# A decoder layer with an expert gather: output products of the first token tile pulled ahead, the second group's depthwise convolution moved to ScalarE and GpSimd, its output products spaced out

## What is computed

```
h = x + W_out( concat[A, B, C, D]( rmsnorm(x) @ W_in ) )
x = h + PEER( rmsnorm(h) )                     then a final rmsnorm
A  convolution group: GLU, causal depthwise conv of width 31 over 256 channels, layernorm, swish
B  RWKV-7 time mixing (state update over chunks of 64 tokens)
C  short gated convolution, width 3
D  multi-scale causal pooling
PEER: 8 heads; for each token and head the 16 best of 128 x 128 product keys pick 16 experts;
      out = sum over the 128 picked experts of gate * gelu(u . x) * v,   u, v rows of 1024
```

## Time and profile before

| | |
|---|---|
| median of 3 runs | 1740.42 us (1735.06 to 1740.69) |
| the profiled execution | 1737.21 us |
| its span | 1735.4 us |
| DVE busy | 1269.9 us (73%) |
| PE busy | 1238.7 us (71%) |
| POOL busy | 911.6 us (53%) |
| ACT busy | 698.1 us (40%) |
| moved by DMA | 602.42 MB, 545.29 MB of it by GpSimd's gathers |
| chain that ended last | DMA 39%, PE 25%, DVE 16%, POOL 6%, issue 6%, ACT 4% |

### The profile page before, as it was taken

How to read it: one execution, slowest core, us unless ns; L and a number is a source line. 1 busy time by engine, 2 the same in 40 slices (tenths; PEclk the granted TensorE clock), 3 DMA queues, 4 the chain that set the end, 5 groups by cost and what they waited for, 6 DMA issues and landing times.

```text
span 1735.4 us, 19464 instructions
## 1 busy us (share of the span) xinstructions
PE 1238.7 (71%) x5360; PEld 623.9 (36%) x5360; DVE 1269.9 (73%) x2983; ACT 698.1 (40%) x1986; POOL 911.6 (53%) x1134
## 2 busy tenths in 40 slices
PE   5997898667767777767976757676767667677555
PEld 4886766323334343332322413232323223222110
DVE  3569755689888878768586778777777777777775
ACT  3321113455444444334345444343434343434444
POOL 0155120476676556544365656565656565556652
PEclk9999898878899898887987878787877787867778
DMA  5321147999999999999799999999999999999996
GB/s 173 122 100 47 37 138 95 319 397 412 418 410 416 417 405 419 417 418 392 260 374 417 419 417 419 415 401 417 417 409 404 418 411 418 409 408 410 418 419 254
DMA packets 110636, 602.42 MB, mean 347 GB/s; under 512 B 24752, under 2 KB 27184, under 8 KB 43968
## 3 DMA queue, kind: packets, MB, share of 16 engines
q0 software_dynamic: 74880, 545.29, 76.8%
q1 hardware_dynamic: 35648, 55.90, 11.0%
HBM read 597.96 MB, written 3.19 MB: 346 GB/s over the span
## 4 chain that ended last, share of the span: by engine, by line
DMA 39%; PE 25%; DVE 16%; POOL 6%; issue 6%; ACT 4%; DVEq 3%; POOLq 0%; SPq 0%; ACTq 0%
DMA arena<-in_uv,arena 38%; PE ps L981 9%; DVE arena L1844 8%; PE ps L551 4%; POOL arena L2068 4%; DVEq L1313 3%; DVE arena L1316 3%; PE ps L598 2%; POOL arena L2067 2%; PE ps L904 2%; DVE arena L1322 2%; PE ps L589 2%; PE ps L611 1%; ACT arena L1280 1%; PE ps L923 1%
## 5 line engine op out<-in xcount | busy, mean ns | idle before, releaser
L981 PE MATMUL ps<-arena 128*64 128x512 f32 x2048 | 666.9, 785 | 402.7 <-ACT arena L1280 401.8
L1844 DVE CUSTOM_DVE_ANT_0 arena<-arena 128x1024 f32<-128x1024 f32 x520 | 639.1, 1230 | 276.7 <-DMA arena<-in_uv,arena 247.5
L2068 POOL DMA_INDIRECT arena<-in_uv,arena x520 | 617.9, 1188 | 89.3 <-POOL arena L2067 17.2
L2067 POOL TENSOR_TENSOR arena<-arena 1x1 f32<-1x1 f32 x520 | 211.6, 407 | 539.3 <-PE ps L981 404.9
L981 PEld LDWEIGHTS ps<-arena 128*64 128x64 f32 x2048 | 153.7, 165 | 788.7 <-ACT arena L1280 469.4
L1274 ACT ACTIVATE arena<-arena 128x1 f32<-128x1 f32 x520 | 105.4, 203 | 759.7 <-DVE arena L1844 755.5
L1280 ACT ACTIVATE arena<-arena 128x64 f32<-128x64 f32 (+1 forms) x520 | 181.4, 349 | 17.0
L1276 ACT ACTIVATE arena<-arena 128x1 f32<-128x1 f32 x520 | 153.2, 295 | 16.9
L1316 DVE TENSOR_TENSOR arena<-arena 128x512 f32<-128x512 f32 (+7 forms) x310 | 132.5, 428 | 28.5 <-ACT arena L1028 18.9
L904 PEld LDWEIGHTS ps<-arena 128*128 128x128 f32 x1024 | 127.8, 206 | 39.7 <-issue 38.0
L551 PE MATMUL ps<-arena 128*128 128x264 f32 (+1 forms) x608 | 141.5, 388 | 0.7 <-DVE arena L1316 0.7
(11 more groups left out here) (161 smaller groups left out, 965.0 us busy)
## 6 DMA issues: line engine op xcount, KB each, us to landing
arena<-in_win SPq DMA_DIRECT2D x38, 512.0 KB, 3.2
arena<-in_wqk SPq DMA_DIRECT2D x64, 256.0 KB
arena<-in_uv,arena POOLq DMA_INDIRECT x520
arena<-in_wout SPq DMA_DIRECT2D x16, 512.0 KB, 3.9
arena<-in_xp SPq DMA_DIRECT2D x4, 512.0 KB, 7.2
arena<-in_wqk SPq DMA_DIRECT2D x16, 128.0 KB
out_yp<-arena SPq DMA_DIRECT2D x4, 512.0 KB
arena<-in_const SPq DMA_DIRECT2D x1, 928.0 KB, 4.5
```

What stands on the lines that cost most here:

```text
L981: last = mm(ps[64 * q:64 * q + 64, b + c, :], diag[:, (s + q) % 8, :], ring[:, (s + q) % RING, D + 512 * c:D + 512 * c + 512], start=(s == ...
L1844: v.tensor_tensor_reduce(out=ring[:, s % RING, 0:D], in0=ring[:, s % RING, 0:D], in1=row, scale=1.0, scalar=0.0, op0=MUL, op1=ADD, accum_o ...
L2067: pool.tensor_tensor(carrier[:, 1:2], carrier[:, 0:1], carrier[:, 0:1], ALU.add).then_inc(S["carried"], 1)
L2068: pool.indirect_dma_start(out=ring[:, s % RING, :], out_offset=None, in_=a["uv"][:, :], in_offset=bass.IndirectOffsetOnAxis(ap=idx[:, t, s ...
```

## The change

Four things are done.

1. **Order of the front.** Output products go tile by tile: `first_out(t, lo, hi)` takes blocks lo to hi for one tile, so the 8 weight blocks are loaded twice (54 blocks in place of 46). Tile 0 is finished first, then normalised, transposed and queried; then the last five z columns, the second half of tile 1's products, its norm, transposes, query and score. VectorE does `choose(0, ...)` before `residual(1)`. GpSimd starts the gathers when tile 0's indices are there; slot 2 waits for tile 0's copies, slot 4 for the last z column, slot 6 for tile 1's products. The first group of state outputs is issued after block 45, the load of the keys is mixed with the blocks.
2. **Convolution of group 1.** ScalarE makes the 31 products (`products`, two scaled copies each, ring of three), GpSimd adds them up (`second_convolution`, 14 before `windows_second`, 17 after). VectorE only does group 0.
3. **Mean, variance, root, scaling and swish of that convolution** move into `mixer(1)`, ticks 0 to 9, so into unit 0. TensorE's unit 1 waits for its root.
4. **Output products of group 1** go from ticks `C_OUT` + 0, 1, 3, 4, 6, 7 to `C_OUT` + 0, 3, 6, 9, 12, 15, norms and transposes behind them accordingly; SyncE's load of each of the eight `w_blocks` waits for slots 164, 166, ... 178.

The diff, cut to its core:

```diff
+BLOCKS = z_blocks(0, ZFRONT) + out_blocks(0, 0, 2) + z_blocks(ZFRONT, ZFRONT + 1) + out_blocks(0, 2, 6) + z_blocks(ZFRONT + 1, ZFRONT + 2) \
+    + out_blocks(0, 6, 8) + out_blocks(1, 0, 4) + z_blocks(ZFRONT + 2, len(ZORDER)) + out_blocks(1, 4, 8)
+W_SLOT = 164
...
             for n in range(n_out + 5, len(BLOCKS)):
                 weights(n)
-                if n == n_out + 8:
+                k = n - n_out - 5
+                if k < 4:
+                    sp_.dma_start(wqk[:, 512 * k:512 * k + 512], a["wqk"][0][:, 512 * k:512 * k + 512]).then_inc(d_wqk, 16)
...
+                if n == n_out + 14:
...
                     for j in range(KT):
+                        sp_.wait_ge(S["slot_used"], W_SLOT + 2 * j)
                         sp_.dma_start(w_blocks[j], a["wout"][:, OUT_ORDER[j], :]).then_inc(d_wb, 16)
...
+            def first_out(t, lo, hi):
+
+                for j in range(lo, hi):
+                    n = BLOCK_OF[("out", KT * t + j)]
+                    pe.wait_ge(d_w[n % 3], 16 * (n // 3 + 1))
...
                     for nh in range(2):
+                        last = mm(ps[:, (2, 5)[t] + nh, :], ya[:, OUT_ORDER[j], 128 * t:128 * t + 128], w[:, 512 * nh:512 * nh + 512],
                                   start=(j == 0), stop=(j == KT - 1))
...
+                if g:
+                    yield E_XS
+                    conf_mean(1)
+                    yield E_XS + 2
+                    conf_variance(1)
...
+                for k in range(3):
+                    yield C_OUT + 6 * k
                     project(k, 0)
+                    yield C_OUT + 6 * k + 3
                     project(k, 1)
...
             first.until(C_LN)
             pe.wait_ge(S["pool_out"], 4)
+            first_out(0, 0, 2)
+            zcol()
+            first.finish()
             pe.wait_ge(S["short_done"], 1)
             pe.wait_ge(S["conf_out"], 1)
+            first_out(0, 2, 6)
             zcol()
+            pe.wait_ge(S["rwkv_out"], 1)
+            first_out(0, 6, 8)
+            first_out(1, 0, 4)
+            turned(0, 0)
+            turned(0, 1)
...
             query(0)
             score(0)
+            zcol(len(ZORDER) - zn[0])
+            first_out(1, 4, 8)
+            turned(1, 0)
+            turned(1, 1)
             query(1)
             score(1)
...
+            def products(count):
+
+                for _ in range(count):
+                    m = made[0]
+                    if m == CK:
+                        return
+                    if m == 0:
+                        act.wait_ge(S["glu_done"], 2)
+                    if m >= 3:
+                        act.wait_ge(S["tap_added"], m - 2)
+                    for cc in range(2):
+                        last = f(product[m % 3][:, cc, :], gpad[:, cc, GT + m:2 * GT + m], ACT.Copy, scale=col("cw", CK * cc + m))
+                    last.then_inc(S["tap_ready"], 1)
+                    made[0] += 1
...
                 shifted(0, 1)
                 yield E_XS + 1
+                if g:
+                    conf_center(1)
                 shifted(1, 3)
...
             for step in range(STEPS - 1):
                 choose(0, step)
             lk(v.memset(sscore[0:64], 0.0))
+            residual(1)
+            choose(0, STEPS - 1)
+            second_mean(1)
+            second_norm(1)
+            second_features(1, 0)
+            second_features(1, 1)
             for step in range(STEPS):
                 choose(1, step)
-                if step == 2:
-                    choose(0, STEPS - 1)
...
+            def second_convolution(lo, hi):
+
+                for m in range(lo, hi):
+                    pool.wait_ge(S["tap_ready"], m + 1)
+                    if m:
+                        pool.wait_ge(S["tap_added"], m)
+                    tt(cacc[1], cacc[1] if m else cb, product[m % 3], ADD).then_inc(S["tap_added"], 1)
...
+            second_convolution(0, 14)
             windows_second()
+            second_convolution(14, CK)
             short(1)
```

More of the change, by code:

```diff
@@ L133, with out_blocks, z_blocks @@
 OUT_ORDER = (6, 7, 4, 5, 0, 1, 2, 3)
-BLOCKS = [("z", j) for j in range(ZFRONT)] + [("out", j) for j in range(KT)] + [("z", j) for j in range(ZFRONT, len(ZORDER))]
+def out_blocks(t, lo, hi):
+    return [("out", KT * t + j) for j in range(lo, hi)]
+def z_blocks(lo, hi):
+    return [("z", j) for j in range(lo, hi)]
+BLOCKS = z_blocks(0, ZFRONT) + out_blocks(0, 0, 2) + z_blocks(ZFRONT, ZFRONT + 1) + out_blocks(0, 2, 6) + z_blocks(ZFRONT + 1, ZFRONT + 2) \
+    + out_blocks(0, 6, 8) + out_blocks(1, 0, 4) + z_blocks(ZFRONT + 2, len(ZORDER)) + out_blocks(1, 4, 8)
 BLOCK_OF = {b: n for n, b in enumerate(BLOCKS)}
@@ L181, with TURN_BANK @@
 POOL_AHEAD = 10
+def TURN_BANK(t, half):
+    return 4 if (t, half) == (0, 1) else 7
 PE_AHEAD = 3
+W_SLOT = 164
 def pace(k):
@@ L307, in build @@
         cacc = (at(o_p + 1084, 2, GA), yb[:, 2:4, 0:GT])
-        csq = at(o_r + 2816, 2, GA)
+        product = [at(o_p + 7 * NT + 512 * (i + 1), 2, GT) for i in range(3)]
+        csq = (at(o_r + 2816, 2, GA), product[0])
         ctmp = at(o_r + 2816, 2, NS, CK)
@@ L784, in turned @@
-                def turned(k, half):
-                    t = tiles[k]
-                    pe.wait_ge(S["xn2_done"], t + 1)
-                    if 2 * t + half:
-                        pe.wait_ge(S["hT2_done"], 2 * t + half)
-                    turn_half(t, half, 7)
-                for k in range(2):
-                    yield C_OUT + 3 * k
+                        pe.wait_ge(S["rwkv_out"], 2)
+                        pe.wait_ge(d_wb, 16 * KT)
+                        if k:
+                            pe.wait_ge(S["x1_done"], t)
@@ new lines, in mixer, with turned @@
+                yield C_OUT + 28
+                pe.wait_ge(S["hT2_done"], 2 * TILES + 2)
+                for n_ in range(2):
+                    last = mm(ps[:, 5 + n_, :], cst("sel")[0:NS, :], xn2[TILES][0:NS, 512 * n_:512 * n_ + 512], start=True, stop=True)
+                last.then_inc(S["xrep_mm"], 1)
+            def turned(t, half):
+                pe.wait_ge(S["xn2_done"], t + 1)
+                if 2 * t + half and (t, half) != (0, 1):
+                    pe.wait_ge(S["hT2_done"], 2 * t + half)
+                turn_half(t, half, TURN_BANK(t, half))
@@ L1199, in _ @@
                 zc()
+                if lv >= 3:
+                    products(2)
                 first.until(base + 8)
@@ L1214, in _ @@
                 zc()
+                products(2)
                 first.until(C_CH + 6 * c + 4)
-            first.until(C_LN + 4)
-            first.until(C_OUT + 3)
+                products(3)
             zc()
-            conf_root(1)
             first.finish()
-            conf_sigmoid(1)
+            zc()
+            second_squares(0)
+            root(0, "mean2", 1, "root2")
             def queries(v):
@@ new lines, in mixer @@
+                yield C_OUT + 17
+                residual(TILES)
+                second_features(2, 0)
+                yield C_OUT + 19
+                second_mean(TILES)
+                second_features(2, 1)
+                yield C_OUT + 21
+                second_features(3, 0)
+                yield C_OUT + 22
+                second_norm(TILES)
+                yield C_OUT + 23
+                second_features(3, 1)
+                yield C_OUT + 25
+                second_features(TILES, 0)
```

300 lines of the change are left out of this document (122 added, 178 removed).

## The result

The changed kernel took **1760.8 us** (median; 1755.6 to 1764.8) against 1740.6 for the kernel before beside it: a ratio of 1.012, 95% interval 1.010 to 1.014. It is slower by some 20 us, above the range of the prediction (1720 to 1754). The profiled execution took 1760.6 us, span 1758.5.

The account below looks back on a forecast made before the run. Expert-row gathers keep the DMA engines busy in the steady stretches, so only the front and the 800 to 880 us dent matter. Front +15.4 and dent -14.3 sum to +1: 1739 us, 8 in 10 within 1720 to 1754.

Parts of the forecast that it names:

- The front up to 235.6 us: Stretch before tile 0's output products, with the convolution moved to ScalarE and GpSimd: cost 0, from -3 to +4 us.
- Tile 0: Tile 0's products to its selection: scores at 274.4 instead of 291.56, first gather about 286.5 instead of 305.01.
- Tile 1's products: Five z columns, then four output blocks of tile 1: products end between 304.5 and 312, taken as 306.
- From there to the first dot product: Tile 1's norm, transposes, query, score and selection: selection starts at 322.9, first dot at 336.5 instead of 320.25.
- The restart: First dot to slot 12, VectorE waiting for conf_mean(1): slot 12 lands at 368.0 against 352.6; front costs 15.4 us.
- The rest of the convolution's tail: VectorE work and extra tables in units 0 and 1: hidden by the ring, 0; 5 if the cover fails.
- The dent: DMA dip from 800 to 880 us, second group's output products spread: gives back 14.3 us (11.3 to 16.3).
- (b): Rival: tile 1's chain and the last weight block's wait at slot 179; +9, about 1749 us; chance 0.27.
- worst case of 23 us: Front's upper cost: tile 1's products end at 312 and the query takes 6.8 us.
- (a): Rival: front costs little, weights among gathers come at once; -6 to -10, about 1729 us; chance 0.36.
- (c): Rival: no gain in the dent, front's 15 stands alone, 1754 us; chance within (b)'s.
- in_nf's 12.9: Landing time in us of the only 512 KB load issued among gathers, used as evidence for late weight blocks.

Follow-up runs that it names:

- e2: Changed kernel with conf_mean(1), the second convolution's channel mean, done before unit 0 instead of behind unit 2's query; 1756.3 us, ratio 1.010.
- e8: e7 plus the whole tail of the second convolution's norm moved from units 0 to 1 into the front's idle time; 1743.8 us, ratio 1.003.
- e7: Changed kernel with all five small-packet outputs issued only when tile 1's output products are done; 1751.1 us, ratio 1.007.
- e13: Changed kernel with o_spool, o_ssc and o_sconf issued between 170 and 200 us, where the DMA engines are nearly idle; 1752.4 us, ratio 1.006.
- e14: e9 with e13's edit, the three outputs issued between 170 and 200 us; 1720.7 us, ratio 0.989.
- e1: Changed kernel with the three state outputs (o_swkv, o_sconf, o_spool) issued after the last weight block; 1753.8 us, ratio 1.008.
- e11: Kernel before with spread products, front's idle time used, tile 1's selection in unit 0, and all five small-packet outputs behind the last z block; 1759.7 us, ratio 1.010.
- e3: Changed kernel with GpSimd's first gather held until tile 1's output products are done; 1759.7 us, ratio 1.012.
- e4: Kernel before with only the second group's output products spread and their weight blocks issued one per pair of slots; 1724.8 us, ratio 0.992.
- e16: e10 with e13's edit, the three outputs issued between 170 and 200 us; 1716.9 us, ratio 0.986.
- e9: e8 with tile 1's last output blocks ahead of z columns 34 to 38 and its norm between steps of tile 0's selection; 1749.9 us, ratio 1.006.
- e10: e9 plus tile 1's selection between the dot products of unit 0; 1759.9 us, ratio 1.012.

## Why the prediction was wrong

**The front up to 235.6 us**: right. F is 237.0 (236.6 before). ScalarE did wait for GpSimd as forecast, and TensorE was not later for it (171.58 against 175.91):

```profile
170.14 0.91 ACT L1076 ACTIVATE arena<-arena 128x256 f32<-128x256 f32 x2 [9.48 <-POOL arena L1925]
```

**Tile 0**: 3.5 us optimistic. Scores at 277.9 for 274.4, first gather 290.2 for 286.5.

**Tile 1's products**: the step that failed first, out_mm 2 at 321.5 for 306. Of these 15.5 us, 3.5 are tile 0's. I let the small packets hold the second z column until 282; it started at 288.42: 2.9 more. The four z columns from there took 18.7 us for 13.9, with a second wait of 1.69 and the clock down to 0.81 between 290 and 300 us after the idle time: 4.8. The four output blocks took 14.4 for 10.1 (wait 5.19, the last at 3.48 instead of 1.9): 4.3. Each had been seen, and each was taken near its cheap end. In the range I had let them go wrong one at a time (312 at worst), but one delay feeds the next: late packets, an idle TensorE, a lower clock, gathers that meanwhile are under way.

**From there to the first dot product**: right, 29.9 us for 30.5 (321.5 to 351.38).

**The restart**: the second step that failed. The forecast had the first dot product 16.3 us late and slot 12 15.4, a gain of 1; measured were 31.1, 38.3 at slot 12 and, from slot 16 on, 39.2, a loss of 8.1. From the first dot product to slot 12 I had 31.5 us with VectorE's wait for the mean and 26 without; it was 40.8. The wait itself had the right length (9.38 for 8 to 9), but the sum charged 5.5 for it and e2 got 7.8 back: 2.3. The rest of the convolution's tail was costed at 0 with 5 as the price if the cover fails. The cover failed: conf_scale(1) stands between slots 11 and 12, where the transfers have only just begun again, and slot 12's dot product came 4.6 us after its rows. With the whole tail in the front (e8) the stretch took 31.3 us, and 29 without the 2 us that are e7's new wait: 4 less than e2, about the 5 named as a price. The last 3 us, 29 against the 26 forecast for a restart without any of this, no run takes apart.

**The dent**: right, 15.4 us for 14.3. TensorE waited 2.37 us for a weight block instead of 7; the blocks took 7.7 to 9.0 us from issue to landing (median 8.0):

```profile
851.39 7.11 PE L619 MATMUL ps<-arena 128*128 128x512 f32 x16 [2.37 <-DMA arena<-in_wout]
...
arena<-in_wout SPq DMA_DIRECT2D x8, 512.0 KB, 8.0
```

**The rivals**. (b) had the sign, but its mechanism (the block at slot 179) was worth 2 us; the loss came from tile 1's chain, whose worst case of 23 us was set too low. (a) and (c) are out. The Trainium skill's rule (DMA: Bandwidth & Descriptors, "Queues, rings and completion order"), that a DMA engine takes turns between queues packet by packet, would by the prediction's estimate give some 4 us for a block beside gathers; I had set in_nf's 12.9 against it. Neither was the price of a block: the eight of the second group took 7.7 to 9.0 us to land, the last three of e13 7.3, 8.5 and 10.6. What the trace has at 4 us is the distance between blocks when three are under way (e13's products start 4.1, 4.6 and 3.8 us apart). That is twice what a block used for 1.7 us can bear, so even as a distance the 4 us speak against the rival.

**What the front's 38 us consist of** (F to slot 12's dot product, 155.2 against 117.3), by the runs, each built on the one before: 8.9 for the small packets (e7, 146.3), 7.0 for the convolution's tail (e8, 139.3) and 27.8 for the order (e14, 111.5), together 43.7, since e14 ends 6 us ahead of before. e14 also has the three outputs elsewhere, which by e13 against e7 (144.8 and 146.3) is worth 1.5. Taken singly from the changed kernel the outputs gave 11.3 (e1) and the mean 7.8 (e2). The order alone was not run on the changed kernel. I had priced the order as if tile 1 were late by its own z columns alone; it is late by everything that those columns wait for.

## What to carry to other kernels

Handing one tile's result over early gains nothing while an engine's fixed order makes the consumer wait for the other tile: look for the last of the results that stand ahead of the first release of a buffer, and move work that this result doesn't need (here 17 us of z columns) behind it. Place outputs of many small packets where the DMA engines are idle and no load is queued, and look up who waits for their landing before moving them. A term that is "hidden by the ring" is hidden only while slots have landed ahead.

## What the runs showed of the hardware

Three outputs of 2048 packets are cheap in bytes (376 KB together) and dear in time. In e11 SyncE was 11.86 us at the issue of o_spool and 18.10 at that of o_tails behind it, so o_ssc was issued at 335.86 only, and it landed 19.9 us later. TensorE and VectorE stood for 38 us:

```profile
317.00:355.00 38.00, 0.00 (x0) 0.00 (x0) 0.00 (x0) 1.26 (x4) 4.29 (x7) 0.54 1.16 157
```

The Trainium skill (DMA: Bandwidth & Descriptors, "Specifications") puts full rate at transfers of 512 bytes and more, with a read-modify-write below. The trace agrees in direction: in e13 from 172 to 186 us, with the packets and two weight blocks under way, the engines are busy 0.76 of the time for 50 GB/s; in after, with plain loads alone from 186 to 200 us, 0.16 for 51.

F lay at 241.4 us in e1, 240.1 in e2 and 238.6 in e3 and at 237.0 in the changed kernel, though none of the three edits touches anything ahead of it. The difference is there before 50 us, in the first two z columns, where the same matmuls ran slower. In e13 the granted clock was 0.57 from 19 to 23 us, where it was 1.00 in after; in e1 it reads 1.00 there too, so the clock's rows do not explain it in every kernel.

```profile
19.00:23.00 4.00, 4.00 (x12) 3.13 (x12) 0.00 (x0) 0.00 (x0) 0.00 (x0) 0.57 0.75 166
```

The medians went along: e1's gain of 11.3 us behind F is 7.0 in the time, e2's of 7.8 is 4.5. Time less the stretch from F to slot 12 is 1604.5 to 1606.5 us in the six kernels that have the spread and an F below 238.2, and 1607.0 to 1610.9 in the eight with one above 239. So it isn't only a matter of the one profiled execution. Whether it belongs to the build or to the chip is not shown: e1 to e4 ran on one chip and e13 to e16 on another, and all eight were late; but e11 was late on the chip where e9 and e10 were not. In e2 and e13 the profiled execution was also 3.2 and 4.6 us above its kernel's median. A change of 3 us at the end says little until F is looked at.
